# ScalarE copies the turned softmax weights of one unit ahead of the exponential of the next

## The reference

```python
log_f = log_sigmoid(f_logit + b_forget)
c = cumsum(log_f)
s = q @ k.T * scale + c[query] - c[key]
s = where(key <= query, s, -inf)
out = softmax(s) @ v
```

## Time and profile before

| | us |
|---|---|
| median of 3 runs | 2734.89 |
| lowest and highest of them | 2731.26, 2737.59 |
| the profiled execution, its own time | 2734.06 |
| its span in the trace | 2732.8 |
| first attention, about | 137 to 474 in the span |
| TensorE matmul busy | 2610.9 (96%) |
| VectorE busy | 1855.1 (68%) |
| ScalarE busy | 1310.4 (48%) |

### The profile page before, as it was taken

The page is one execution under the profiler, slowest core; times in us unless marked ns, Lnnn a source line. Parts: engine busy times, 40 slices in busy tenths (PEclk is TensorE's granted clock), DMA queues, the critical chain, the costliest instruction groups (busy, mean ns, idle before and its releaser), DMA issues. The chain is left out here.

```text
span 2732.8 us, 35908 instructions
## 1 busy us (share of the span) xinstructions
PE 2610.9 (96%) x13421; PEld 2204.2 (81%) x13421; DVE 1855.1 (68%) x2321; ACT 1310.4 (48%) x2014; POOL 483.1 (18%) x665
## 2 busy tenths in 40 slices
PE   8989989999999999999999999989998599999996
PEld 7788888888898877777888898878877488888885
DVE  4378887742337888885556433389845788888887
ACT  4255554331235333333435312178833377777775
POOL 6711110000003232222001320012232300000102
PEclk9999999999999999999999999999999799999998
DMA  8700010121323455556764532001234699999998
GB/s 306 254 24 13 13 35 17 48 61 47 117 84 105 130 160 167 183 190 245 236 201 149 145 73 69 13 20 25 77 132 161 237 375 396 394 396 395 395 395 278
DMA packets 249516, 461.90 MB, mean 169 GB/s; under 512 B 16589, under 2 KB 138177, under 8 KB 247937
## 3 DMA queue, kind: packets, MB, share of 16 engines
q1 hardware_dynamic: 218944, 352.73, 36.8%
q0 software_dynamic: 30288, 106.84, 11.9%
q10 hardware_dynamic: 112, 0.03, 0.0%
HBM read 384.79 MB, written 65.32 MB: 165 GB/s over the span
## 5 line engine op out<-in xcount | busy, mean ns | idle before, releaser
L508 PE MATMUL ps<-r,r 128*128 128x512 f32 (+4 forms) x10508 | 2304.8, 377 | 10.5 <-DVE r L672 3.8
L508 PEld LDWEIGHTS ps<-r,r 128*128 128x128 f32 (+1 forms) x10508 | 1881.7, 189 | 363.1 <-issue 12.4
L485 ACT ACTIVATE r<-f 128x2048 fp32r<-128x2048 f32 (+2 forms) x339 | 503.8, 1494 | 385.6 <-PE ps L508 379.2
L3740 DVE TENSOR_TENSOR r<-f,r 128x2048 fp32r<-128x2048 f32 x188 | 429.3, 2291 | 63.7 <-ACT r L485 62.5
L493 DVE TENSOR_TENSOR r<-f,r 128x1024 fp32r<-128x1024 f32 (+1 forms) x151 | 168.0, 1126 | 314.1 <-ACT r L485 314.1
L508 PE MATMUL ps<-f,f 128*128 128x128 f32 (+1 forms) x1218 | 153.5, 277 | 0.3 <-DVE f L3688 0.3
L876 DVE SCALAR_TENSOR_TENSOR f<-f,misc,f 128x1023 f32<-128x1023 f32 (+29 forms) x120 | 147.9, 1258 | 0.0
L508 PEld LDWEIGHTS ps<-f,f 128*128 128x128 f32 x1218 | 145.7, 194 | 1.4 <-DVE f L3688 0.5
L2019 ACT ACTIVATE r<-f 128x512 fp32r<-128x512 f32 x140 | 87.1, 629 | 70.8 <-PE ps L508 58.9
L3758 POOL DMA_INDIRECT ff_scratch<-f,misc x15 | 28.8, 1919 | 474.4 <-ACT f L3869 412.2
L3270 DVE TENSOR_REDUCE misc<-ps 128x1 f32<-128x1280 f32 x64 | 95.1, 1487 | 21.6 <-PE ps L508 21.2
(11 more groups left out here) (350 smaller groups left out, 2237.1 us busy)
## 6 DMA issues: line engine op xcount, KB each, us to landing
f<-in_w_gate_dram SPq DMA_DIRECT2D x64, 1024.0 KB, 8.4
f<-in_w_up_dram SPq DMA_DIRECT2D x64, 1024.0 KB, 10.5
f<-in_w_down_dram SPq DMA_DIRECT2D x64, 1024.0 KB, 8.2
f<-in_w_in_dram SPq DMA_DIRECT2D x56, 512.0 KB, 4.3
f<-in_w_ada_dram SPq DMA_DIRECT2D x96, 256.0 KB, 4.7
f<-in_w_ffn_in_dram SPq DMA_DIRECT2D x80, 256.0 KB, 4.1
hid_scratch<-f POOLq DMA_DIRECT2D x77, 256.0 KB, 2.8
f<-hid_scratch SPq DMA_DIRECT2D x35, 512.0 KB, 5.0
```

What stands on the lines that cost most here:

```text
L485: self.act.activation(hi, raw, ACT.Copy).then_inc(self.sem(st.name + "_hi"), 1)
L508: return self.pe.matmul(o, left, right, start=start, stop=stop, skip_group_check=True)
L3740: self.dve.tensor_tensor(es.lo[i % 4], es.raw[i % 8], es.hi[i % 4].bitcast(F32), ALU.subtract).then_inc(self.sem("e_lo"), 1)
```

## The change

In every step the two calls change places in ScalarE's list: the copy of the turned weights of unit u - 1 now stands before the exponential of unit u. No instruction is added, removed or resized, and no wait is edited; the other engines' lists stay as they are. (The second copies of the high parts, in `act_copy_qk`, stay on ScalarE.)

```diff
@@ act_attention
             g, u = self.unit(s, 3)
             if g is not None and u % 2:
                 self.act_copy_o(g, u)
+            g, u = self.unit(s, 1)
+            if g is not None:
+                self.act_copy_p(g, u)
             g, u = self.unit(s, 0)
             if g is not None:
                 self.act_exp(g, u)
-            g, u = self.unit(s, 1)
-            if g is not None:
-                self.act_copy_p(g, u)
             g, t = self.tile(s, 2)
             if g is not None:
                 self.act_values(g, t)
```

## The result

| | median, us | lowest to highest | ratio to before, 95% |
|---|---|---|---|
| kernel before | 2735.9 | 2731.26 to 2737.59 | |
| kernel after | 2720.72 | 2714.57 to 2727.59 | 0.9946, 0.9925 to 0.9966 |

The change makes the kernel about 15 us faster, 0.54%. The prediction was 2723.3.

A forecast was written before the change was run, and what follows sets the result against it. TensorE, busy 307.58 of 337 us in the first attention, was taken as the bound, idling for ScalarE's order. Group gains 3.0, 4.1, 3.6, 0.9 make 11.6: 2734.06 to 2722.5 us, median 2723.3; range 2714 to 2731.

The forecast's parts named there:

- The mechanism: First attention: copy L1234 starts within 0.05 us of part 0's end; L1225's waits fall from 22.8 to below 3 us.
- 1 or 2: VectorE's waits before L1241 forecast to fall from some 7 us in a group to this many us.
- The narrow steps: Steps without part 1: delayed exponential and values copy lose 0.09, 0.29, 0.48 us in steps 4, 6, 8; 0.85 per group.
- The rule that spoke against the change: ScalarE's queue is first in, first out: a waiting copy holds a ready exponential; step 8 priced at 0.48 us.
- The wide steps: Second group, steps 9 to 0 of the next: TensorE's advance grows to 4.95 us, even steps held by the values copy.
- The waits that came back: L1127 waits for values copy L1077 0.5 to 1 us in steps 10, 12, 14; some 8 to 11 us in all.
- waits for L1077 beyond 15 us: Sign of being wrong: TensorE's waits for the values copy growing past that size would point to rival 3.
- rival 3: Wide even steps pay up to 0.48 us per tile behind the copy; 9.4 us lost, 2743.5 us; chance 0.07.
- The groups: First attention's four groups gain 3.0, 4.1, 3.6 and 0.9 us, together 11.6 us.
- rival 1: Low-clock stretches go with the idle time: first three groups gain more, together 14.5 us, 2719.6 us; chance 0.18.
- low stretches that move: Sign of being wrong: TensorE's low-clock stretches in the first attention move or multiply.
- Rival 2: VectorE does not follow, its taps and low parts set the maximum: 1.4 us gained in all, 2732.7 us; chance 0.13.

The follow-up runs named there:

- Experiment 3: Against the kernel before: copy ahead of the exponential only in the wide units (8 to 15), old order in the narrow ones; 2716.61 us, ratio 0.9937.
- experiment 2: The kernel before once more, unchanged, for a second profile; 2730.42 us.
- the two repeats: The kernel before once more, 2730.42 us, and the kernel after once more, 2719.66 us, each with a second profile.
- experiment 4: Against the kernel before: copy ahead of the exponential only in the narrow units (below 8), old order in the wide ones; 2737.55 us, ratio 1.0014.
- the third profile: The kernel after, unchanged, profiled a third time in a single run; 2722.01 us.
- experiment 5: Against the kernel before: copy ahead of the exponential only for wide units in odd steps (9, 11, 13, 15); 2723.72 us, ratio 0.9963.
- experiment 1: The kernel after once more and a third time, unchanged; 2719.66 us, ratio 0.9945, and 2722.01 us in the single run.

## Why the prediction was right, and where its terms were off

*The mechanism.* It held at each step that the prediction named. L1225's waits went from 22.8 us to none. The copy starts 0.04 us behind part 0, and in step 8 the exponential and the values copy stand 0.48 and 1.26 us behind it, as forecast. VectorE's waits before L1241 in the first three groups are 0.5, 2.1 and 0.5 us, down from 7.0, 6.7 and 6.9; of the 13.6 in all 10.5 lie in the last group, which had 13.2 before and did not fall to "1 or 2".

*The narrow steps.* Forecast: losses of 0.09, 0.29 and 0.48 us, 0.85 with the rounding, in steps 4, 6 and 8. The marks of the second group stand 7.27, 8.07 and 9.24 us apart in the kernel after and 7.21, 7.80 and 8.75 before: 0.06, 0.27 and 0.49. Experiment 3 gives 0.92 for a group. The rule that spoke against the change, the strict first in, first out of ScalarE's queue in the Trainium skill, "PSUM — Partial Sum Buffer", section "Engine vs sequencer instructions", is borne out by these rows: the exponential had its input and stood behind a copy that had not, 0.49 us in step 8.

*The wide steps.* Forecast against experiment 3, as the advance over the kernel before since the mark at 249.58 (254.82 before). The last column is the same for the third group, against the kernel before of experiment 2, since the clock was low in that group of the first profile:

| after step | forecast | second group | third group |
|---|---|---|---|
| 10 | 0.71 | 0.97 | 0.95 |
| 12 | 3.12 | 2.77 | 3.59 |
| 14 | 4.56 | 4.92 | 5.02 |
| 0 of the next group | 4.95 | 5.54 | 5.63 |

The term is 0.6 too small. A likely part of it: the working took part 1 to start at the end of the matmuls before it, but an unblocked turn starts 0.16 us before that end, so each bracket under-read what the wait had cost. In the four odd steps, where part 1 sets how far TensorE is, that would be 4 x 0.16 = 0.64 us; in the even ones the values copy sets the next start. That this comes near 0.6 is arithmetic, and the surplus doesn't grow evenly over these steps. Something that the working left out shows in the second group alone: I followed the exponential and the copies, and not the high parts that stand between them and wait for a DMA. Behind them the values product waits for L1291, 1.31 us in the second group of experiment 3 and about 0.45 in the two others. It sets the mark of step 12 back by 0.8, but at the end of the group nearly nothing is left of it, 5.54 against 5.63: in the third group L1127 has a wait of 1.19 us after step 14 instead, where the second has 0.57.

*The waits that came back.* Forecast 8 to 11 us for L1127, measured 15.3. In the wide steps they are as forecast, 8.6 us in all; in the second group of experiment 3 they are 0.68, 0.56, 0.57 and 0.51 us, 2.3 where 2.9 were forecast. The forecast had not counted the 0.36 and 0.56 us of the narrow steps, 3.7 in all, though it had priced them, nor the 0.2 to 0.3 at each step 2 (1.0 in all) and the 2.1 of the attention's second tile, which were there before. So one of its signs of being wrong, waits for L1077 beyond 15 us, came in without the rival 3 that it stood for: the sum of a wait's rows was compared with a sum over part of its places. Rival 3, which forecast a loss, is refuted by the result, and by experiment 3, where the wide steps alone gain 17 us.

*The groups.* Forecast 3.0, 4.1, 3.6 and 0.9, in all 11.6. By the two repeats it was 4.64, 4.64, 4.83 and 1.69, in all 15.8. Of the difference of 4.2 us 0.6 a group is the wide steps' term. I took 3.0 for the first group since I expected its low clock to stay and to show, and 3.6 for the third since its waits were fewer at the low clock; without a low clock both gain as the second does. The 0.8 of the last group are not explained. In the profiled execution of before the first group took 85.00 us, 1.24 more than the undisturbed 83.76, and the kernel after took 79.15: 5.85 gained. That is rival 1, and it is half right. By the number it even comes nearer than the forecast: its 2719.6 us leaves out the 0.8 that the forecast adds for the median (as the times of the other rivals do), so 2720.4, and 2720.72 was measured. Part of that is luck. It takes 4.1 for a group, and the second group gains 4.64 with the clock at full on both sides (83.68 in the first profile of the kernel before, 79.04 in the repeat of the kernel after), which no rival forecast.

*Rival 1 and the clock.* Behind the wait of 1.8 us in step 11 the clock fell in six of nine groups that had it: two of the kernel before, one in its repeat, all three of experiment 4. With that wait gone it fell after step 11 or 12 in one of the 30 groups so profiled (the first three of ten profiles), the second of the kernel after, and there behind the new wait of 1.75 us. The prediction's sign of being wrong, low stretches that move, is thus there in the first profile of the kernel after (from 192 and 357 to 270 and 456) and in neither of the two others. But the length of the wait doesn't decide it: in the third profile of the kernel after it stayed at full behind the wait of 1.95 us, and in experiment 5 behind three waits of 1.8 us in step 14.

What a low stretch costs depends on the waits that follow it. In the old order they hide most of it, as the prediction said: 1.24 us in the first group of the kernel before, 0.17 in its third (83.80 against 83.63), nothing in the second of its repeat. In experiment 4 the groups take 85.91, 84.51 and 85.65 us, where the undisturbed 83.7 and the narrow steps' 0.85 make 84.5: 1.4, nothing and 1.1. In the new order it shows. The second group of the kernel after takes 81.91 us, the third profile with a longer wait there 79.66: 2.25 us or more. At the end of the attention, where the wait of the earlier trace rows grew from 1.24 to 1.85 us, a second one cost 3.2 us (164.81 us from the last mark to the first L1480, against 161.58 in the repeat with the same wait). This is why the profiled executions are 9.3 us apart at the first L1480 (561.82 and 552.57) where the repeats are 15.3. So a removed wait gave back its length, and between nothing and 1.4 us more where the clock had fallen behind it.

The forecast was 2.6 us too high: its gain was 3.6 too small, and the median before came out 1.0 higher with five runs than with three. The groups' terms above are enough for that; how much of it the clock adds over many executions these profiles don't say.

*Rival 2.* Refuted: VectorE idled less, and experiment 5 shows the maximum of step 12 coming earlier, at 272.24 with part 0 at 273.07, where the earlier trace rows have it 0.65 us behind part 0's start. Ahead of it only steps 9 and 11 of the group had been changed.

*What stays open.* That the 0.16 us explains the wide steps' surplus was not tested alone. Why the clock falls behind a wait of 1.8 us in one group and not in the next isn't settled by these runs. The later stages don't carry the whole distance to the end in every execution. Between the repeats it is 15.3 us at the first L1480, 13.8 near 1990 and 9.7 at the end; between the first two profiles 9.3, 9.3 and 6.4. In the repeat of the kernel after the granted clock is 0.79, 0.72 and 0.76 in 1985 to 1993, 2017 to 2023 and 2089 to 2096, where that of the kernel before has 1.00 from 1990 to 2100. The medians, 15 us apart in the result and 14 in experiment 1, say that this isn't the rule, but what sets it is open.

## What to carry to other kernels

In an engine that works strictly in order, put first the instruction whose result another engine waits for soonest, not the one that has waited longest; then look at what now stands behind it, and at the next such result (here the values copy, worth another 8 us). Split such a change by size of work: where the second part of the turning did not exist the new order only cost, and the version for wide units alone is 3 us better by its median, 0.9 us a group by its marks. An engine that runs earlier meets its loads earlier, so follow every entry of its list, the ones that wait for DMA too.

## What the runs showed of the hardware

The start of a matmul group that nothing blocks lies 0.16 us before the end that the trace gives the group ahead of it (260.94 against 261.10, and 0.15 to 0.17 in 48 of 49 such rows of two profiles), so an idle bracket before such a turn under-reads the wait by about that much. The Trainium skill, "Perfetto Trace Analysis", section "Tensor Engine Instruction (MATMUL, LD_WEIGHTS)", says that the profiler estimates a matmul's end from its size and doesn't observe it; the trace agrees.

The granted clock fell to the lower of its levels, 1.2 GHz (0.50 in a whole window at 456), behind waits of 1.75 to 1.85 us in part of the cases (six of nine in step 11 of the old order, four of nine at the end of the attention), stayed at full behind one of 1.95 us and three of 1.8 us, and did not fall behind the waits of 0.5 to 0.7 us that took their place. The same is seen at the start of the attention: behind the wait of 2.07 us of its second tile the clock of 138 to 144 is 0.78 in the kernel after and its repeat, and 1.00 in the profiled execution of before, which had the same wait.
